# The first block's values taken from X before the norm, the normalised operand made beside them from the turned X

## The chip, the core and the metric

The kernel runs on one core of one Trainium2 chip. The metric is the device time of one execution, in microseconds (us). The kernel before took 1599.45 us, the median of three runs (1598.53 to 1599.94).

## The reference, cut to what matters

The network is a first block (mixer of mLSTM heads and a gated MLP, cross attention, a mixture of experts, final norm) followed by two layers of a second block, on 256 rows of 1024 numbers. All of the change lies in the first microseconds of the first block. There the reference computes

```
h    = x * rsqrt(mean(x*x, axis=-1) + eps) * g_mix      # 256 x 1024
proj = h @ w_in                                         # 1024 x PROJ_COLS
v    = proj[:, 1024:1536]                               # values, 4 heads of 128
gates = proj[:, 2048:2064]                              # and q, k, o, u, v of the gated MLP
```

The factor rsqrt(...) is one number for each row of x, so it can be taken out of the product: v = rsqrt(...) * ((x * g_mix) @ w_in).

## The kernel before, in words

Every engine has a program written out by hand; Python functions named after the engine emit it (tensor_mixer, scalar_mixer, vector_mixer, gpsimd_start, sync_start), and the order of the calls is the order of the work on that engine. Nothing reorders it. Engines wait on each other by counting semaphores (`e.wait_ge(*s.name[event])`). All instructions pass through a small class Port, so the profile shows its lines: L172 matmul, L175 transpose, L178 activation on ScalarE, L184 tensor_tensor, L187 tensor_scalar, L190 scalar_tensor_tensor, L217 a DMA issue. Groups are told apart by the names of tiles.

The weights come as a stream of chunks of 128 x 1024 numbers, two to a unit of 1 MB, from `in_ws_dram` into a ring of seven units (RING). A product in 32 bits is made of three reduced-precision ones. For this ScalarE copies each chunk, rounded, to WH ("hi", hi_half), and VectorE subtracts it from the chunk to give the rest in RINGL ("lo", lo_half); chunks 1 and 3 have their rest made on GpSimd (LOW_ON_POOL). The activations are split in the same way: HA (hi, from ScalarE) and LA (lo, from VectorE). TensorE then does hi*hi, hi*lo and lo*hi.

The first norm: the sum of squares of a tile of 128 rows is taken half on ScalarE (mean_square), half on VectorE (vector_square). VectorE adds them (rstd_mean), ScalarE takes log and exponential (rstd_root), VectorE does one Newton step in two instructions (rstd_step, rstd_last: the two `SM<-SM` of L190, together rstd_end) and puts the root on a diagonal matrix DIAG (rstd_diagonal). TensorE multiplies X by DIAG (norm_turn), which turns and normalises it at once, eight products for each tile t of 128 rows, four to a PSUM bank. norm_hi and norm_lo take HA and LA from these banks, with the gain g_mix as a scale by partition, from the parameters PARS.

The values (chunks 0 to 3) are computed in tiles: stream_tile(c0, j, t) is chunk j for rows t, six products of 512 columns. After the eight such groups come chunk 4 (the gates, stream_t: eight steps of three products of 256 columns), and chunk 5, before which TensorE also waits for the constants. From there on the stream of chunks goes on without a pause for a long time. SyncE issues the DMAs in one order (sync_start): X tile 0, the identity, PARS, unit 0, X tile 1, unit 1, unit 2, the memory, unit 3, the other constants, units 4 to 6; unit 7 and later wait for a chunk of the ring to be used up.

Chunks 0 and 1 are unit 0, chunks 2 and 3 unit 1, chunks 4 and 5 unit 2.

Of the kernel before, what the change touches and what calls it, by code (L numbers as in the profile page):

```python
# [38 lines left out]
_n = 0  # L39
for _name, _w in [("g_mix", 8), ("g_mem", 8), ("g_xattn", 8), ("g_moe", 8), ("conv_w", 40),  # L40
                  ("conv_b", 8), ("g_head", 4), ("gate_b", 1), ("br", 1),
# [598 lines left out]
def fetch(e, m, s, A, u):  # L640

    if u == U_B2:
        w = m.slot[m.home[u]]
        e.dma_start(w[:, 0:1024], A["ws"][u][:, 0:1024]).then_inc(*s.first_in.up(0))
# [284 lines left out]
def sync_start(e, m, s, A):  # L929
    e.dma_start(m.X[:, 0, :], A["x"][0]).then_inc(*s.x_in.up(0))  # L930
    e.dma_start(m.CONS[:, 0:128], A["con"][:, 0:128]).then_inc(*s.ident_in.up(0))
    e.dma_start(m.PARS[:, :], A["par"]).then_inc(*s.par_in.up(0))
# [42 lines left out]

def tensor_mixer(e, m, s):
    a = normed(s, "mix", m.HA, m.LA)
    norm_turn(e, m, s, "mix", m.X, 0)
    for j in range(3):
        stream_tile(e, m, s, 0, j, 0, a, None)  # L980
    norm_turn(e, m, s, "mix", m.X, 1)
    stream_tile(e, m, s, 0, 3, 0, a, (s.evac, ("v", 0)))
    for j in range(4):
        stream_tile(e, m, s, 0, j, 1, a, (s.evac, ("v", 1)))
# [421 lines left out]
def vector_mixer(e, m, s):  # L1406
# [12 lines left out]
    norm_lo(e, m, s, "mix", m.HA, m.LA, "g_mix", 0, 0)
    e.wait_ge(*s.x1_in[0])  # L1420
    vector_square(e, m, s, 1)
    norm_lo(e, m, s, "mix", m.HA, m.LA, "g_mix", 0, 1)
    lo_half(e, m, s, 2)
    e.wait_ge(*s.square["mix", 1, 0])
    e.wait_ge(*s.square_v[1])
    rstd_mean(e, m, s, "mix", 1)
    rstd_end(e, m, s, "mix", 1)
    rstd_diagonal(e, m, s, "mix", 1)
    lo_halves(e, m, s, 4, 6)
    norm_lo(e, m, s, "mix", m.HA, m.LA, "g_mix", 1, 0)  # L1430
    norm_lo(e, m, s, "mix", m.HA, m.LA, "g_mix", 1, 1)
# [3006 lines left out]
```

## Time and profile before

| what | value |
|---|---|
| median of three runs | 1599.45 us |
| time of the profiled execution | 1598.25 us |
| its span in the profile | 1596.4 us |
| TensorE busy with products | 1558.0 us (98%) |
| VectorE, ScalarE, GpSimd busy | 952.6, 692.8, 63.8 us |
| the chain that ended last | TensorE 84%, DMA 10%, VectorE 4%, ScalarE 2% |

The span is what the profile covers; the time of the same execution is 1.85 us longer. Busy time counts the time in which an engine works on an instruction. The chain is followed back from the last instruction to whatever released each step.

### The profile page before, as it was taken

The numbers are of one execution on the slowest core, as the hardware profiler recorded it, in microseconds if no ns is written. First come the engines' busy times: TensorE is split into PE (matmuls) and PEld (weight loads), VectorE is DVE, ScalarE is ACT, GpSimd is POOL, SyncE is SP. The second block draws the span as 40 slices with busy tenths as digits, with TensorE's granted clock in tenths as the row PEclk, the third lists the DMA queues.
The fourth block names the chain that finished last, engine by engine and source line by source line (L and its number), as shares of the span: only waits on it lengthen the run. The fifth ranks groups of instructions, "written<-read, shape, count | busy, mean of one in ns | idle before, by whom it ended". The sixth has DMA issues, their size and how long they took to land.

```text
span 1596.4 us, 22640 instructions
## 1 busy us (share of the span) xinstructions
PE 1558.0 (98%) x9209; PEld 1178.2 (74%) x9209; DVE 952.6 (60%) x1636; ACT 692.8 (43%) x1229; POOL 63.8 (4%) x68
## 2 busy tenths in 40 slices
PE   7999999999999999999999999999999999999998
PEld 6997885443433433448997889999899978899997
DVE  5967655222333233237788667766767885677666
ACT  6765542111010110136664446554655644465544
POOL 1010000000000000003001000000030010000000
PEclk9999999999999999999999999999999999999999
DMA  9443477999999999996345545555453445455550
GB/s 367 170 148 132 177 324 297 410 423 424 423 424 423 422 424 424 424 420 214 133 146 179 179 160 214 186 186 187 169 185 133 172 158 184 173 198 185 185 185 27
DMA packets 57246, 398.87 MB, mean 250 GB/s; under 512 B 6352, under 2 KB 6736, under 8 KB 10036
## 3 DMA queue, kind: packets, MB, share of 16 engines
q1 hardware_dynamic: 56706, 395.63, 64.2%
q8 instruction: 73, 1.20, 0.3%
q10 hardware_dynamic: 434, 1.77, 0.3%
q14 instruction: 33, 0.27, 0.1%
HBM read 396.33 MB, written 1.05 MB: 249 GB/s over the span
## 4 chain that ended last, share of the span: by engine, by line
PE 84%; DMA 10%; DVE 4%; ACT 2%; issue 1%; SPq 0%; DVEq 0%; ACTq 0%
PE P L172 82%; DMA ew<-in_ws_dram 8%; PE P L175 2%; DMA ez<-in_ws_dram 1%; DVE RINGL L184 1%; ACT WH L178 0%; DMA RING<-in_ws_dram 0%; DVE LA L190 0%; SPq L217 0%; ACT HA L178 0%; DVE SM L190 0%; DVE YB L184 0%; DVE PXP L190 0%; ACT JNK L178 0%; ACT L181 0%
## 5 line engine op out<-in xcount | busy, mean ns | idle before, releaser
L184 DVE TENSOR_TENSOR RINGL<-RING,WH 128x1024 fp32r<-128x1024 f32 x347 | 421.9, 1240 | 104.7 <-ACT WH L178 103.4
L178 ACT ACTIVATE WH<-RING 128x1024 fp32r<-128x1024 f32 x351 | 356.5, 1053 | 49.9 <-PE P L172 47.5
L172 PE MATMUL P<-HA,WH 128*128 128x256 f32 x1208 | 345.4, 286 | 0.0
L172 PE MATMUL P<-LA,WH 128*128 128x256 f32 x1208 | 340.3, 282 | 0.0
L172 PE MATMUL P<-HA,RINGL 128*128 128x256 f32 x1208 | 340.3, 282 | 0.0
L172 PEld LDWEIGHTS P<-HA,WH 128*128 128x128 f32 x1208 | 227.7, 189 | 5.6 <-issue 3.0
L172 PEld LDWEIGHTS P<-HA,RINGL 128*128 128x128 f32 x1208 | 228.4, 189 | 1.9
L172 PEld LDWEIGHTS P<-LA,WH 128*128 128x128 f32 x1208 | 228.6, 189 | 0.0
L172 PE MATMUL P<-WH,HA 128*128 128x512 f32 x368 | 148.1, 402 | 1.8 <-ACT VN L178 1.3
L172 PE MATMUL P<-RINGL,HA 128*128 128x512 f32 x368 | 145.7, 396 | 1.8 <-POOL RINGL L184 1.4
L172 PE MATMUL P<-WH,LA 128*128 128x512 f32 x368 | 144.9, 394 | 0.5 <-DVE LA L190 0.4
L172 PE MATMUL P<-RING,XT 128*64 128x512 f32 x536 | 122.3, 594 | 4.0 <-DMA RING<-in_ws_dram 4.0
L184 DVE TENSOR_TENSOR GS<-P,GS 128x512 f32<-128x512 f32 x16 | 11.1, 692 | 175.3 <-PE P L172 175.3
L172 PEld LDWEIGHTS P<-RING,XT 128*64 128x64 f32 x536 | 37.6, 137 | 82.5 <-issue 67.4
L190 DVE SCALAR_TENSOR_TENSOR YSL<-P,SM,YSH 128x512 fp32r<-128x512 f32 x32 | 22.6, 747 | 121.9 <-ACT YSH L178 121.9
L172 PEld LDWEIGHTS P<-WH,HA 128*128 128x128 f32 x368 | 69.4, 188 | 18.4 <-ACT WH L178 1.7
L172 PEld LDWEIGHTS P<-RINGL,HA 128*128 128x128 f32 x368 | 69.5, 189 | 18.0 <-POOL RINGL L184 1.8
L172 PEld LDWEIGHTS P<-WH,LA 128*128 128x128 f32 x368 | 69.3, 188 | 17.4 <-DVE LA L190 1.5
L172 PE MATMUL P<-ew,XT 128*64 128x512 f32 x304 | 71.4, 596 | 6.8 <-DMA ew<-in_ws_dram 6.8
L178 ACT ACTIVATE HT<-P 128x512 f32<-128x512 f32 x16 | 9.6, 598 | 155.9 <-PE P L175 155.9
L178 ACT ACTIVATE YSH<-P,SM 128x512 fp32r<-128x512 f32 x32 | 20.4, 684 | 130.7 <-PE P L172 130.7
L172 PE MATMUL P<-WH,FL 128*128 128x512 f32 x176 | 69.8, 396 | 0.0
(411 smaller groups left out, 2431.6 us busy)
## 6 DMA issues: line engine op xcount, KB each, us to landing
RING<-in_ws_dram SPq DMA_DIRECT2D x279, 1024.0 KB, 4.9
ew<-in_ws_dram SPq DMA_DIRECT2D x42, 1024.0 KB, 23.6
ez<-in_ws_dram SPq DMA_DIRECT2D x15, 1024.0 KB, 20.5
ek<-in_ws_dram SPq DMA_DIRECT2D x11, 1024.0 KB, 18.2
ef<-in_ws_dram SPq DMA_DIRECT2D x8, 1024.0 KB, 12.8
eha<-in_ws_dram SPq DMA_DIRECT2D x4, 1024.0 KB, 9.3
ela<-in_ws_dram SPq DMA_DIRECT2D x3, 1024.0 KB, 6.9
ewr<-in_ws_dram SPq DMA_DIRECT2D x3, 1024.0 KB, 13.8
```

The source lines that it names most:

```text
L172: return self.engine.matmul(*a, **k) if self.engine else self
L175: return self.engine.transpose(*a) if self.engine else self
L178: return self.engine.activation(*a, **k) if self.engine else self
L184: return self.engine.tensor_tensor(*a) if self.engine else self
L190: return self.engine.scalar_tensor_tensor(*a) if self.engine else self
```

## The change

The values are computed from X itself, turned with the identity (raw_turn, transposes instead of products with DIAG) and multiplied by the gain, split into HB and LB (first_hi, first_lo). The root is applied when the values leave PSUM, as a scale by partition (scalar_values). Both tiles are turned before chunk 1, and the groups of the values alternate between the tiles: v(0,0), turn of tile 1, v(1,0), v(0,1), v(1,1), v(2,0), spread, v(2,1), v(3,0), v(3,1).

All that follows (chunk 4 on) still reads the normalised HA and LA. They are now made from the same PSUM banks: two small products (spread_root) of a matrix of ones with DIAG put the roots of all 256 rows on every partition, ScalarE copies them to RB0, VectorE multiplies the turned X by gain and RB0 into QK (first_normal, 16 instructions in 4 groups), ScalarE rounds QK to HA (first_normal_hi, 4 instructions of 128 x 512), and GpSimd subtracts to give LA (first_normal_lo, 4 instructions of 128 x 512). Chunk 1's rest moves from GpSimd to VectorE; chunk 3's stays on GpSimd.

The gain moves from PARS to a place beside the identity, so both come in one DMA. Units 0 and 1 are fetched in halves, each chunk with a semaphore of its own; the ones (64 KB) and PARS come behind unit 1.

```diff
@@ sync_start @@
-    e.dma_start(m.CONS[:, 0:128], A["con"][:, 0:128]).then_inc(*s.ident_in.up(0))
-    e.dma_start(m.PARS[:, :], A["par"]).then_inc(*s.par_in.up(0))
+    e.dma_start(m.CONS[:, 0:136], A["con"][:, 0:136]).then_inc(*s.ident_in.up(0))
     fetch(e, m, s, A, 0)
     e.dma_start(m.X[:, 1, :], A["x"][1]).then_inc(*s.x1_in.up(0))
     fetch(e, m, s, A, 1)
+    e.dma_start(m.CONS[:, 136:264], A["con"][:, 136:264]).then_inc(*s.ones_in.up(0))
+    e.dma_start(m.PARS[:, :], A["par"]).then_inc(*s.par_in.up(0))
     fetch(e, m, s, A, 2)
...
@@ gpsimd_start @@
-    lo_half(e, m, s, 1)
     lo_half(e, m, s, 3)
+    first_normal_lo(e, m, s, 0, 0)
+    first_normal_lo(e, m, s, 1, 0)
+    first_normal_lo(e, m, s, 0, 1)
+    first_normal_lo(e, m, s, 1, 1)
@@ new functions @@
+def first_normal(e, m, s, t, i):
+    ta = slice(t * 128, (t + 1) * 128)
+    e.wait_ge(*s.evac["spread", "mix"])
+    for q in range(4):
+        k = 4 * i + q
+        p = e.scalar_tensor_tensor(m.QK[:, k, ta], m.P[4 + 2 * t + i][:, q * 128:(q + 1) * 128],
+                                   m.con("gain", k, k + 1), m.RB0[:, ta], ALU.mult, ALU.mult)
+    p.then_inc(*s.normal.up(t, i))
+def first_normal_hi(e, m, s, t, i):
+    ta = slice(t * 128, (t + 1) * 128)
+    e.wait_ge(*s.normal[t, i])
+    e.activation(m.HA[:, 4 * i:4 * i + 4, ta], m.QK[:, 4 * i:4 * i + 4, ta],
+                 ACT.Copy).then_inc(*s.norm_hi.up("mix", t, i))
+def first_normal_lo(e, m, s, t, i):
+    ta = slice(t * 128, (t + 1) * 128)
+    e.wait_ge(*s.norm_hi["mix", t, i])
+    e.tensor_tensor(m.LA[:, 4 * i:4 * i + 4, ta], m.QK[:, 4 * i:4 * i + 4, ta],
+                    plain(m.HA[:, 4 * i:4 * i + 4, ta]), ALU.subtract).then_inc(*s.normal_lo.up(t, i))
...
@@ tensor_mixer @@
+    raw_turn(e, m, s, "mix", 0, [(s.x_in, (0,))] * 2)
+    v(0, 0)
+    raw_turn(e, m, s, "mix", 1, [(s.x1_in, (0,))] * 2)
...
+    v(2, 0)
+    e.wait_ge(*s.ones_in[0])
+    spread_root(e, m, s, "mix", 3)
+    v(2, 1)
+    v(3, 0)
+    v(3, 1)
+    a = Operand(m.HA, m.LA, lambda k, t: (s.norm_hi, ("mix", t, k // 4)), lambda k, t: (s.normal_lo, (t, k // 4)))
     stream_t(e, m, s, 4, a, (s.evac, ("gate", 3)))
@@ scalar_mixer @@
+    first_hi(e, m, s, 0, 0)
+    hi_halves(e, m, s, 0, 2)
+    first_hi(e, m, s, 0, 1)
     mean_square(e, m, s, "mix", 0, 0)
+    e.wait_ge(*s.x1_in[0])
+    e.wait_ge(*s.square["mix", 0, 0])
+    mean_square(e, m, s, "mix", 1, 0)
+    first_hi(e, m, s, 1, 0)
+    rstd_root(e, m, s, "mix", 0)
+    rstd_root(e, m, s, "mix", 1)
+    hi_half(e, m, s, 2)
+    first_hi(e, m, s, 1, 1)
+    hi_halves(e, m, s, 3, 5)
+    e.wait_ge(*s.product["spread", "mix", 1])
+    e.activation(m.RB0[:, :], m.P[m.bank["spread", "mix"]][:, 0:256], ACT.Copy).then_inc(*s.evac.up("spread", "mix"))
+    hi_half(e, m, s, 5)
+    first_normal_hi(e, m, s, 0, 0)
+    first_normal_hi(e, m, s, 1, 0)
+    scalar_values(e, m, s, 0)
+    first_normal_hi(e, m, s, 0, 1)
+    first_normal_hi(e, m, s, 1, 1)
+    hi_half(e, m, s, 6)
+    scalar_values(e, m, s, 1)
+    hi_halves(e, m, s, 7, 9)
@@ scalar_values @@
+    e.wait_ge(*s.scale["mix", t])
     e.activation(m.V1[:, t, :, 0:128], m.P[m.bank[0, t]][:, :].rearrange("p (h d) -> p h d", h=4),
-                 ACT.Copy).then_inc(*s.evac.up("v", t))
+                 ACT.Copy, scale=m.SM[:, 12 + t:13 + t]).then_inc(*s.evac.up("v", t))
@@ vector_mixer @@
     vector_square(e, m, s, 0)
+    first_lo(e, m, s, 0, 0)
+    lo_halves(e, m, s, 0, 2)
+    first_lo(e, m, s, 0, 1)
...
+    vector_square(e, m, s, 1)
...
+    first_lo(e, m, s, 1, 0)
+    lo_half(e, m, s, 2)
+    for t in range(2):
+        rstd_end(e, m, s, "mix", t)
+        vector_scale(e, m, s, "mix", t)
+        rstd_diagonal(e, m, s, "mix", t)
+    first_lo(e, m, s, 1, 1)
+    lo_half(e, m, s, 4)
+    first_normal(e, m, s, 0, 0)
+    first_normal(e, m, s, 1, 0)
+    first_normal(e, m, s, 0, 1)
+    first_normal(e, m, s, 1, 1)
     e.wait_ge(*s.par_in[0])
-    lo_half(e, m, s, 0)
...
+    lo_half(e, m, s, 5)
     lo_halves(e, m, s, 6, 10)
```

What GpSimd has at the start of its program before, behind five memsets (RINGL is a chunk's rest, GV belongs to a much later part):

```order
L214 MEMSET NC 128x512
L184 ISA
L184 TENSOR_TENSOR RINGL<-RING,WH 128x1024 [waits hi] x2
L184 TENSOR_TENSOR GV<-GV,LNG 128x512 [waits ln_g_in,vec]
L184 TENSOR_TENSOR GV<-GV,LNB 128x512 [waits gained,ln_b_in]
```

And now:

```order
L214 MEMSET NC 128x512
L184 ISA
L184 TENSOR_TENSOR RINGL<-RING,WH 128x1024 [waits hi]
L184 TENSOR_TENSOR LA<-QK,HA 128x4x128 [waits norm_hi] x4
L184 TENSOR_TENSOR GV<-GV,LNG 128x512 [waits ln_g_in,vec]
L184 TENSOR_TENSOR GV<-GV,LNB 128x512 [waits gained,ln_b_in]
```

One of the two subtractions of a chunk has left, and four of half the size, on the operand of chunk 4, stand behind the other.

VectorE from the rest of chunk 2 to the rest of chunk 5 in the changed kernel (SM<-SM are the steps of the root, tile 0 and then tile 1):

```order
L184 TENSOR_TENSOR RINGL<-RING,WH 128x1024 [waits hi]
L190 SCALAR_TENSOR_TENSOR SM<-SM 128x1 [waits root]
L190 SCALAR_TENSOR_TENSOR SM<-SM 128x1 [waits rstd]
L187 TENSOR_SCALAR SM<-SM 128x1 [waits rstd]
L187 TENSOR_SCALAR DIAG<-CONS,SM 128x128
L190 SCALAR_TENSOR_TENSOR SM<-SM 128x1 [waits root]
L190 SCALAR_TENSOR_TENSOR SM<-SM 128x1 [waits rstd]
L187 TENSOR_SCALAR SM<-SM 128x1 [waits rstd]
L187 TENSOR_SCALAR DIAG<-CONS,SM 128x128
L190 SCALAR_TENSOR_TENSOR LB<-P,CONS,HB 128x128 [waits norm_hi]
L190 SCALAR_TENSOR_TENSOR LB<-P,CONS,HB 128x128 x3
L184 TENSOR_TENSOR RINGL<-RING,WH 128x1024 [waits hi]
L190 SCALAR_TENSOR_TENSOR QK<-P,CONS,RB_90 128x128 [waits evac]
L190 SCALAR_TENSOR_TENSOR QK<-P,CONS,RB_90 128x128 x15
L184 TENSOR_TENSOR RINGL<-RING,WH 128x1024 [waits hi,par_in]
```

Both roots now stand together, and behind them wait the rest of tile 1's second half, the rest of chunk 4 and the sixteen products that make the normalised operand; before, the second root stood behind the rest of chunk 2, and two subtractions of chunks and eight instructions of LA followed it.

## Rows read from the trace of the kernel before

**Rows 1.** The page: busy time, share of the span, instructions.
```profile
PE 1558.0 (98%) x9209; PEld 1178.2 (74%) x9209; DVE 952.6 (60%) x1636; ACT 692.8 (43%) x1229; POOL 63.8 (4%) x68
```
**Rows 2.** Chain of waits, in order: start us, us, what.
```profile
19.12 60.86 PE P L172 x438
...
428.28 26.48 DMA ew<-in_ws_dram
```
**Rows 3.** Who waited for whom on SyncE's DMA queue, whole span: total, times, longest.
```profile
SPq L217 <- PE P L172: 1344.5, 348, 15.0
```
**Rows 4.** Timeline of TensorE, first 29 us: start, length, instruction, [idle before <-releaser].
```profile
7.42 3.79 PE L172 MATMUL P<-DIAG,X 128*128 128x128 f32 x16 [7.42 <-DVE DIAG L187]
...
12.39 0.63 PE L172 MATMUL P<-WH,HA 128*128 128x512 f32 x1
...
12.82 0.59 PE L172 MATMUL P<-RINGL,HA 128*128 128x512 f32 x1
...
15.24 0.50 PE L172 MATMUL P<-RINGL,HA 128*128 128x512 f32 x1 [1.38 <-POOL RINGL L184]
...
19.12 2.05 PE L172 MATMUL P<-DIAG,X 128*128 128x128 f32 x16 [1.04 <-DVE DIAG L187]
```
**Rows 5.** Stretches: us, TensorE's busy time (instructions), clock, DMA share, GB/s.
```profile
28.01:30.87 2.86, 2.86 (x25) 1.00 0.99 370
```
**Rows 6.** SyncE's timeline at 1.2 us; DMA issues from 1.1 to 1.6: KB, us to landing.
```profile
1.18 0.42 SPq L217 DMA_DIRECT2D CONS<-in_con_dram  x1
...
CONS<-in_con_dram SPq DMA_DIRECT2D x1, 64.0 KB, 3.1
```
**Rows 7.** Timeline, transposes with the identity at 174 us.
```profile
173.93 1.47 PE L175 MATMUL P<-CONS,X 128*128 128x128 f32 x12
```
**Rows 8.** Timeline of ScalarE, VectorE and GpSimd, 6 to 23 us.
```profile
6.16 0.44 ACT L178 ACTIVATE SM<-SM 128x1 f32<-128x1 f32 x2 [1.21 <-DMA PARS<-in_par_dram]
...
6.63 0.41 DVE L190 SCALAR_TENSOR_TENSOR SM<-SM 128x1 f32<-128x1 f32 x2 [1.29 <-ACT SM L178]
...
8.94 1.06 ACT L178 ACTIVATE WH<-RING 128x1024 fp32r<-128x1024 f32 x1 [2.34 <-DMA RING<-in_ws_dram]
...
9.90 1.13 ACT L178 ACTIVATE HA<-P,PARS 128x128 fp32r<-128x128 f32 x4
10.10 1.22 DVE L184 TENSOR_TENSOR RINGL<-RING,WH 128x1024 fp32r<-128x1024 f32 x1 [2.73 <-ACT WH L178]
...
11.24 1.12 DVE L190 SCALAR_TENSOR_TENSOR LA<-P,PARS,HA 128x128 fp32r<-128x128 f32 x4
...
11.51 1.07 ACT L178 ACTIVATE WH<-RING 128x1024 fp32r<-128x1024 f32 x1
...
12.66 2.53 POOL L184 TENSOR_TENSOR RINGL<-RING,WH 128x1024 fp32r<-128x1024 f32 x1 [10.29 <-ACT WH L178]
...
22.61 0.60 ACT L178 ACTIVATE V<-P 128x512 f32<-128x512 f32 x1
```
**Rows 9.** Timeline of GpSimd and VectorE side by side, at 15 and 109 us.
```profile
15.58 2.94 POOL L184 TENSOR_TENSOR RINGL<-RING,WH 128x1024 fp32r<-128x1024 f32 x1 [0.39 <-ACT WH L178]
...
16.90 1.84 DVE L190 SCALAR_TENSOR_TENSOR SM<-SM 128x1 f32<-128x1 f32 x2 [0.50 <-ACT SM L178]
...
109.33 1.50 POOL L184 TENSOR_TENSOR GV<-GV,LNG 128x512 f32<-128x512 f32 x1 [90.80 <-DVE GV L187]
...
109.62 2.29 DVE L184 TENSOR_TENSOR RINGL<-RING,WH 128x1024 fp32r<-128x1024 f32 x1
...
110.97 2.08 POOL L184 TENSOR_TENSOR GV<-GV,LNB 128x512 f32<-128x512 f32 x1
...
111.83 1.11 DVE L190 SCALAR_TENSOR_TENSOR MN<-P,COLS,CONS 128x128 f32<-128x128 f32 x4
...
113.02 1.29 POOL L184 TENSOR_TENSOR GV<-GV,LNG 128x512 f32<-128x512 f32 x1
```
**Rows 10.** All copies of a row of roots from PSUM (tile RB): ns min/median/max.
```profile
L178 ACT ACTIVATE RB<-P x4: 377/378/378, 736.6 to 1414.4; 128x256 f32<-128x256 f32 x4
```

More of the change, by code:

```diff
@@ L39 @@
 _n = 0
-for _name, _w in [("g_mix", 8), ("g_mem", 8), ("g_xattn", 8), ("g_moe", 8), ("conv_w", 40),
+for _name, _w in [("g_mem", 8), ("g_xattn", 8), ("g_moe", 8), ("conv_w", 40),
                   ("conv_b", 8), ("g_head", 4), ("gate_b", 1), ("br", 1),
@@ L53 @@
 _n = 0
-for _name, _w in [("ident", 128), ("ones", 128), ("le", 128), ("ge", 128), ("lt", 128),
+for _name, _w in [("ident", 128), ("gain", 8), ("ones", 128), ("le", 128), ("ge", 128), ("lt", 128),
                   ("mf", 128), ("mb", 128), ("onehot", 512), ("iota", 64), ("cf", 130), ("cb", 130),
@@ L253 @@
 XS = 256 ** -0.5
-CON_WIDTH = {"iota": 64, "onehot": 512, "cf": 130, "cb": 130, "m2": 64, "edge": 64, "lrone": 1}
-LOW_ON_POOL = {1, 3} | {B2 + l * L_CHUNKS + L_AT["ffn"] + 12 for l in range(2)}
+CON_WIDTH = {"iota": 64, "onehot": 512, "cf": 130, "cb": 130, "m2": 64, "edge": 64, "gain": 8, "lrone": 1}
+LOW_ON_POOL = {3} | {B2 + l * L_CHUNKS + L_AT["ffn"] + 12 for l in range(2)}
 EXTRA = ("ek1", "egs", "ez", "ef2", "ef1", "ext", "eha", "ela", "ew0", "ew1", "ew2", "ewr")
@@ L363, in __init__ @@
         self.DN = z("DN", [128, 4])
+        self.RB0 = z("RB0", [128, 128 * 2])
         self.QX = at("QX", [128, 4, 256], Z + 16384)
@@ L602, in __init__ @@
         self.scaled = signal("scaled")
+        self.normal = signal("normal")
+        self.normal_lo = signal("normal_lo")
+        self.ones_in = signal("ones_in", 16)
+        self.second_in = signal("second_in", 16)
         self.norm_lo = signal("norm_lo")
@@ L640, in fetch @@
 def fetch(e, m, s, A, u):
[L642 removed]
+    if u in (0, 1, U_B2):
         w = m.slot[m.home[u]]
[L644 removed]
+        e.dma_start(w[:, 0:1024], A["ws"][u][:, 0:1024]).then_inc(*(s.second_in if u == 1 else s.first_in).up(u))
         e.dma_start(w[:, 1024:2048], A["ws"][u][:, 1024:2048]).then_inc(*s.landed[m.home[u]].up(u))
@@ L805, in norm_lo, with first_hi, first_lo @@
                                plain(hi[:, k, ta]), ALU.mult, ALU.subtract).then_inc(*s.norm_lo.up(tag, t, k))
+def first_hi(e, m, s, t, i):
+    e.wait_ge(*s.turned["raw mix", t, i])
+    for q in range(4):
+        k = 4 * i + q
+        e.activation(m.HB[:, k, t * 128:(t + 1) * 128], m.P[4 + 2 * t + i][:, q * 128:(q + 1) * 128], ACT.Copy,
+                     scale=m.con("gain", k, k + 1)).then_inc(*s.norm_hi.up("raw mix", t, k))
+def first_lo(e, m, s, t, i):
+    ta = slice(t * 128, (t + 1) * 128)
+    e.wait_ge(*s.norm_hi["raw mix", t, 4 * i + 3])
+    for q in range(4):
+        k = 4 * i + q
+        e.scalar_tensor_tensor(m.LB[:, k, ta], m.P[4 + 2 * t + i][:, q * 128:(q + 1) * 128], m.con("gain", k, k + 1),
+                               plain(m.HB[:, k, ta]), ALU.mult, ALU.subtract).then_inc(*s.norm_lo.up("raw mix", t, k))
+def first_normal(e, m, s, t, i):
+    ta = slice(t * 128, (t + 1) * 128)
+    e.wait_ge(*s.evac["spread", "mix"])
+    for q in range(4):
+        k = 4 * i + q
+        p = e.scalar_tensor_tensor(m.QK[:, k, ta], m.P[4 + 2 * t + i][:, q * 128:(q + 1) * 128],
[7 more added lines that the diff above has]
+def first_normal_lo(e, m, s, t, i):
+    ta = slice(t * 128, (t + 1) * 128)
+    e.wait_ge(*s.norm_hi["mix", t, i])
+    e.tensor_tensor(m.LA[:, 4 * i:4 * i + 4, ta], m.QK[:, 4 * i:4 * i + 4, ta],
+                    plain(m.HA[:, 4 * i:4 * i + 4, ta]), ALU.subtract).then_inc(*s.normal_lo.up(t, i))
 def normed(s, tag, hi, lo):
@@ L976, in tensor_mixer @@
 def tensor_mixer(e, m, s):
[L977 to L984, printed above, removed]
+    raw = normed(s, "raw mix", m.HB, m.LB)
+    v = lambda j, t: stream_tile(e, m, s, 0, j, t, raw, (s.evac, ("v", t)))
+    e.wait_ge(*s.ident_in[0])
+    raw_turn(e, m, s, "mix", 0, [(s.x_in, (0,))] * 2)
+    v(0, 0)
+    raw_turn(e, m, s, "mix", 1, [(s.x1_in, (0,))] * 2)
+    for t in range(2):
+        for i in range(2):
+            m.free[4 + 2 * t + i] = [(s.normal, (t, i))]
+    v(1, 0)
+    v(0, 1)
+    v(1, 1)
+    v(2, 0)
[5 more added lines that the diff above has]
+    a = Operand(m.HA, m.LA, lambda k, t: (s.norm_hi, ("mix", t, k // 4)), lambda k, t: (s.normal_lo, (t, k // 4)))
     stream_t(e, m, s, 4, a, (s.evac, ("gate", 3)))
@@ L1410, in vector_mixer @@
     vector_square(e, m, s, 0)
-    e.wait_ge(*s.ident_in[0])
-    e.wait_ge(*s.square["mix", 0, 0])
+    first_lo(e, m, s, 0, 0)
+    lo_halves(e, m, s, 0, 2)
+    first_lo(e, m, s, 0, 1)
+    e.wait_ge(*s.x1_in[0])
     e.wait_ge(*s.square_v[0])
-    rstd_mean(e, m, s, "mix", 0)
-    rstd_end(e, m, s, "mix", 0)
-    rstd_diagonal(e, m, s, "mix", 0)
-    e.wait_ge(*s.par_in[0])
-    lo_half(e, m, s, 0)
[L1419 to L1431, printed above, removed]
+    vector_square(e, m, s, 1)
+    for t in range(2):
+        e.wait_ge(*s.square["mix", t, 0])
+        e.wait_ge(*s.square_v[t])
+        rstd_mean(e, m, s, "mix", t)
+    first_lo(e, m, s, 1, 0)
+    lo_half(e, m, s, 2)
+    for t in range(2):
+        rstd_end(e, m, s, "mix", t)
[7 more added lines that the diff above has]
+    first_normal(e, m, s, 1, 1)
+    e.wait_ge(*s.par_in[0])
+    lo_half(e, m, s, 5)
     lo_halves(e, m, s, 6, 10)
@@ L1439, in vector_mixer @@
         rstd_end(e, m, s, "mem", t)
-        rstd_diagonal(e, m, s, "mem", t, (s.turned, ("mix", t, 1)))
+        rstd_diagonal(e, m, s, "mem", t, (s.product, ("spread", "mix", t)))
     lo_half(e, m, s, 11)
@@ L4383, in vec @@
         par[:v.shape[0], PAR[name]:PAR[name] + v.shape[1]] = v
-    for n in ("g_mix", "g_mem", "g_xattn", "g_moe", "g_head", "conv_w", "conv_b"):
+    con = constants()
+    con[:, CON["gain"]:CON["gain"] + 8] = I["g_mix"][0].reshape(8, 128).T
+    for n in ("g_mem", "g_xattn", "g_moe", "g_head", "conv_w", "conv_b"):
         vec(n, I[n][0])
```

21 lines of the change are left out of this document (3 added, 18 removed).

## The prediction

> **What bounds the kernel now.** First the page: TensorE works 98% of the span, VectorE 60%, GpSimd 4% [rows 1]. An average hides where the change lies, so next the chain of waits. From 19.12 us one piece of 60.86 us hangs on TensorE alone, 438 products without a wait [rows 2]. Whatever makes TensorE enter that piece earlier or later moves all behind it. Further on the chain holds pieces of DMA, such as the 26.48 us at 428 us [rows 2]; but the queue that issues these transfers waits, over the span, 348 times and 1344.5 us for TensorE [rows 3], so a shift at the start moves the transfers too and is neither absorbed nor enlarged there. So the question is one number: when does chunk 5 begin. Chunk 4 takes from 28.01 to 30.87 us, 24 products, 0.119 us each [rows 5]. Chunk 5 now begins at 30.87.
>
> Before that the timeline of TensorE shows the waste that could be won [rows 4]: nothing until 7.42; then products at the low clock, 0.43 us apart for 512 columns (12.39 to 12.82), which is 1.2 GHz, though the clock column of the profile reads 1.00; waits of 1.38 us for GpSimd's rest of chunk 1 and 1.04 us for the second DIAG. At the high level the two turns and 48 products (0.234 us each) need about 15 us of the 20.6 from 7.42 to 28.01.
>
> **The change, step by step.** I follow the new order with durations of the old rows.
>
> *TensorE's start.* The identity is issued at 1.18 and lands 3.1 us later [rows 6]: transposes from 4.3 instead of 7.42. Twelve transposes take 1.47 us, of which the last one's own length is pipelined, so some 0.11 each [rows 7]; at the low level 1.85 times as much, as the two turns of [rows 4] stand to each other (3.79 against 2.05 us): 0.21. The first four are done at 5.15, and another engine sees them some 0.25 later: 5.4. Units in halves and PARS moved behind cost nothing: the first half of unit 0 is needed at 6.4, and lies 1.1 MB behind the queue's start where before the whole unit with PARS lay 1.8 MB behind it and was used at 8.94 [rows 8]; if it came as late as that, the next steps would be 2.5 us later, which I keep as an outer bound. X tile 1, issued right behind, has until 11.0.
>
> *To the second turn.* ScalarE takes four copies of a quarter in 1.0 (9.90 to 10.90; HB like HA): 6.4. It starts chunk 0's rounding, VectorE starts the rest 1.16 after that (8.94 to 10.10 [rows 8]), 7.6, and TensorE can use it 1.3 later: 8.9. Five products at 0.43: 11.05. The second turn's first half and the handover, 0.84 + 0.25: 12.15.
>
> *To the roots.* ScalarE: four copies, 13.2; two roots at 0.46 (row at 6.16 [rows 8]), 14.1; rounding of chunk 2 from 14.1; four copies; rounding of chunk 3 from 16.15. VectorE: rest of chunk 2 from 14.1 + 1.16 = 15.25, for 1.14 (10.10 to 11.24), to 16.4. Then both roots, each two small steps (0.41 [rows 8]) and the scale and diagonal (0.45, from the stretch between the steps and 7.42 plus 0.2 for one more small instruction). The last step of the second root is due at 17.5.
>
> *Where it collides.* GpSimd starts chunk 3's rest 1.15 after ScalarE starts its rounding (11.51 to 12.66 [rows 8]): 17.3, for 2.53. In [rows 9] a small step SM<-SM that came at 16.90 in the middle of such a subtraction (15.58 to 18.52) ran until both were over: 1.84 us for what takes 0.41. So the second root's last step waits until 19.85, and TensorE gets its DIAG at 20.6, having finished v(2,0) before 19. The two products of the spread are four passes of 0.11; with handover and the copy to RB0 (0.38 [rows 10]) the row of roots is there at 21.7. That is hidden: VectorE, from 20.5, has four instructions of LB (1.04: 11.24 to 12.28) and the rest of chunk 4 (1.14) first. The sixteen products of the normalised operand start at 22.7.
>
> *Two engines for one operand.* Each group of four takes 1.04: ends at 23.75, 24.8, 25.8, 26.85. They read PSUM and one tile of SBUF and run beside GpSimd unharmed (MN at 111.83 [rows 9]: 1.11 for four). ScalarE needs 0.6 for 512 columns (V [rows 8]), so GpSimd starts at 24.55. Its piece of 512 takes 1.29 (113.02 [rows 9]); two end at 27.2. VectorE comes with chunk 5's rest at 26.85. In [rows 9] VectorE's rest at 109.62 waited for GpSimd's end at 110.83 and took 2.29 instead of 1.22, then GpSimd's next waited for VectorE and took 2.08 instead of 1.29: they take turns. Hence: VectorE 27.2 to 28.3; GpSimd's third, 29.5; chunk 6's rest, whose rounding ended at 28.6, 30.6; GpSimd's fourth, 31.8. Step 5 of chunk 4 needs it: 10 of the 24 products are left from 31.9, 1.2 us, and **chunk 5 begins at 33.1 instead of 30.87: 2.2 us later**.
>
> *The rest.* The scale on the copy of the values changes no shape: nothing, hidden anyway, since the bank is needed much later. The spread's products and RB0 are counted. Chunk 1's rest on VectorE (1.14) is in the stretch to 11.05, hidden behind TensorE's turn. Behind chunk 5 ScalarE and VectorE have slack as before.
>
> **Sum.** The profiled execution took 1598.25, 1596.4 of it span; with 2.2 more it would be 1600.5. It lies 1.2 below the median of the three runs, so I add to the median: 1599.45 + 2.2 = **1601.7**. Unknown prices at both ends: a piece of LA on GpSimd, which no row shows, lies between 1.15 (the 2.08 row less its wait until 111.9) and 1.5 (the 109.33 row), taken 1.2 to 1.3 from the nearest; at 1.5 all four come 1.0 later, 1602.7, and half a us more if VectorE wins another turn; the order at 17.3 against 17.5 is close: if the small step comes first, DIAG is there at 18.1, but chunk 4's rest, with both inputs in SBUF, waits for GpSimd until 20.2, and all comes only 1.3 earlier: +0.9. The forecast's own range is thus 1600.3 to 1603.2.
>
> **Rivals.**
> *A, slower: the clock falls back.* In the forecast TensorE waits 1.5 us at chunk 4's first step (25.7 to 27.2), then from 28.9 to 31.9. In [rows 4] waits of 1.38 and 1.04 left it at the high level (the second turn took 2.05). It decides whether the wait at step 5 grows to about 3 us. At the start the low level lasted from 7.42 to a little after 12.82, which cost half of that, 2.9; so a fall costs 1.2 (the rest of chunk 4 alone) to 2.9. With 2.3 in between: 1604.0. For it: the longest wait, three in a row (one before the spread too). Against it: no row shows a fall. The Trainium skill's page "TensorE: Matmul & The Clock Gate", section on HAM oscillation, says that waits between bursts of products throw the clock back to half; its Part 4 adds that transposes do not count as work in the same way, which speaks against this change. By that rule the time would be that of this case; no row here shows either.
> *B, about 2 faster: the two engines do not hold each other up.* Then the second DIAG is there at 18.1, the sixteen products start at 20.3 behind chunk 4's rest, GpSimd's four pieces run from 22.15, 1.37 apart, to 27.6, and chunk 5 begins at 28.9: 2.0 earlier, 1597.5. For it: the change gives GpSimd only pieces of half the size. Against it: all three meetings in [rows 9]. The Trainium skill's page "SBUF — State Buffer", section on the two separate sides, has the pair of ports as an exclusive lock taken by whichever starts first; by it this case is out, and the rows agree.
> *C, faster: the operand is ready when TensorE comes.* TensorE alone: from 12.7, 42 products and the spread, 10.3 us, chunk 4 at 23.0, chunk 5 at 25.9: 5 less, 1594.5. For it: it is what is left if TensorE sets the pace, as it does in 98% of the span. Against it: VectorE's and ScalarE's queues add up to 24.5 for the first HA alone.
>
> **Chances.** What a measurement can tell from no change is 0.2%, 3.2 us. Forecast 0.58, of which 0.11 beyond +3.2 (pieces on GpSimd dearer, one more turn of the two engines); A 0.17; B 0.15, of which 0.02 beyond -3.2; C 0.10. So faster 0.12, same 0.60, slower 0.28. The range 1597.4 to 1604.4 takes in B and the middle of A and leaves out C and A's upper half, some 0.18.
>
> **What the profile after would show.** Right: first product at 4.3; GpSimd's chunk 3 at about 17.3 and, inside it, a pair SM<-SM of over 2 us; TensorE idle before the spread; four LA on GpSimd with subtractions RINGL on VectorE in between, each longer than 1.3; TensorE waiting for LA at chunk 4; chunk 5 at about 33. A is seen as products of 256 columns more than 0.2 apart behind such a wait. B is seen as LA pieces of 1.3 in a row beside RINGL of 1.2. The forecast is wrong if chunk 5 begins before 31, or if it begins at 33 and the end does not move with it.

## The result

The changed kernel takes 1603.05 us (median of 13 runs, 1601.5 to 1605.33), the kernel before 1599.45 (13 runs, 1597.96 to 1600.35): ratio 1.0025, 95% interval 1.0018 to 1.0032. That is 3.6 us slower, where 2.2 had been forecast, and a little past the 0.2% (3.2 us) that the prediction took as the least that can be told from no change. The profiled execution took 1603.05 us, 1601.2 of it span. That is 4.8 more than the span before, whose execution lay 1.2 below its median.

The chain of waits of the changed kernel shows where it went (start us, us, what):

```profile
1.66 6.66 DMA RING<-in_ws_dram
...
8.34 1.06 ACT WH L178
...
9.42 1.24 DVE RINGL L184
...
18.97 2.35 DVE SM L190
...
22.72 1.13 DVE RINGL L184
23.85 1.05 DVE QK L190 x4
...
24.92 0.64 ACT HA L178
25.56 0.07 issue
25.63 6.95 POOL LA L184 x4
32.58 0.14 issue
32.72 51.74 PE P L172 x378
```

The long piece on TensorE alone, which began at 19.12 before [rows 2], now begins at 32.72, with 10 products of chunk 4 left. GpSimd, which did not appear on the chain before, holds 6.95 us of it. Chunk 5 starts at 34.99 instead of 30.87 [rows 5].

VectorE, the same timeline as in [rows 8, 9]:

```profile
18.01 0.41 DVE L190 SCALAR_TENSOR_TENSOR SM<-SM 128x1 f32<-128x1 f32 x2
...
18.72 2.58 DVE L190 SCALAR_TENSOR_TENSOR SM<-SM 128x1 f32<-128x1 f32 x2
...
23.77 4.22 DVE L190 SCALAR_TENSOR_TENSOR QK<-P,CONS,RB 128x128 f32<-128x128 f32 x16
27.91 1.31 DVE L184 TENSOR_TENSOR RINGL<-RING,WH 128x1024 fp32r<-128x1024 f32 x1
29.64 5.15 DVE L184 TENSOR_TENSOR RINGL<-RING,WH 128x1024 fp32r<-128x1024 f32 x3 [0.41 <-ACT WH L178]
```

And GpSimd:

```profile
18.89 2.40 POOL L184 TENSOR_TENSOR RINGL<-RING,WH 128x1024 fp32r<-128x1024 f32 x1 [16.53 <-ACT WH L178]
25.63 6.94 POOL L184 TENSOR_TENSOR LA<-QK,HA 128x512 fp32r<-128x512 f32 x4 [4.34 <-ACT HA L178]
```

The first root's pair of small steps takes 0.41, the second's 2.58, and ends when GpSimd's piece ends (21.29). The 2.35 us of the line DVE SM in the chain are thus mostly a wait for GpSimd. It was close: GpSimd's piece began at 18.89, the step that it held up at 18.97. The four pieces of LA take 6.94, and VectorE's three rests beside them 5.15 instead of 3.5 (an estimate from e6, where four take 4.63).

TensorE, the same timeline as in [rows 4]:

```profile
4.40 1.97 PE L175 MATMUL P<-CONS,X 128*128 128x128 f32 x8 [4.40 <-DMA CONS<-in_con_dram]
9.44 0.79 PE L172 MATMUL P<-WH,HB 128*128 128x512 f32 x1 [3.07 <-ACT WH L178]
...
21.74 0.49 PE L172 MATMUL P<-DIAG,CONS 128*128 128x128 f32 x2 [0.78 <-DVE DIAG L187]
...
28.29 0.36 PE L172 MATMUL P<-LA,WH 128*128 128x256 f32 x1 [1.09 <-POOL LA L184]
...
32.72 0.55 PE L172 MATMUL P<-LA,WH 128*128 128x256 f32 x1 [2.76 <-POOL LA L184]
33.07 0.41 PE L172 MATMUL P<-HA,WH 128*128 128x256 f32 x1
33.28 0.41 PE L172 MATMUL P<-HA,RINGL 128*128 128x256 f32 x1
```

TensorE starts 3.0 us earlier, and then waits 3.07 us, until 9.44, for chunk 0's rounding. After the wait of 2.76 the products are 0.21 apart instead of 0.12. The clock column of the stretch 32.72 to 35.42 says the same (columns: TensorE busy (instructions), clock, DMA share, GB/s):

```profile
32.72:35.42 2.70, 2.70 (x13) 0.50 1.01 420
```

The granted clock was 0.50, the level of 1.2 GHz: rival A's mechanism, on top of the forecast's.

### The profile page after: what moved, and what is told of

It is laid out like the page before. It is cut to its first block, busy times and chain, and to the rows that moved or that the text cites. A ratio compares the mean times of both kernels' runs of the same rounds, so it can differ in the third digit from the quotient of the medians.

```text
span 1601.2 us, 22652 instructions
## 1 busy us (share of the span) xinstructions
PE 1559.7 (97%) x9197; PEld 1178.2 (74%) x9197; DVE 959.8 (60%) x1655; ACT 695.1 (43%) x1234; POOL 67.6 (4%) x71
## 4 chain that ended last, share of the span: by engine, by line
PE 83%; DMA 10%; DVE 4%; ACT 2%; issue 1%; POOL 0%; SPq 0%; DVEq 0%; ACTq 0%
PE P L172 81%; DMA ew<-in_ws_dram 8%; PE P L175 2%; DVE RINGL L184 1%; DMA ez<-in_ws_dram 1%; ACT WH L178 0%; POOL LA L184 0%; DMA RING<-in_ws_dram 0%; SPq L217 0%; DVE SM L190 0%; DVE LA L190 0%; DVE YB L184 0%; DVE PXP L190 0%; ACT L181 0%; ACT HA L178 0%
## 5 line engine op out<-in xcount | busy, mean ns | idle before, releaser
L172 PE MATMUL P<-WH,HA 128*128 128x512 f32 x352 | 141.1, 401 | 1.7 <-ACT VN L178 1.3
L172 PE MATMUL P<-RINGL,HA 128*128 128x512 f32 x352 | 138.8, 394 | 0.5 <-DVE RINGL L184 0.5
L172 PE MATMUL P<-WH,LA 128*128 128x512 f32 x352 | 138.3, 393 | 0.5 <-DVE LA L190 0.4
L172 PEld LDWEIGHTS P<-WH,HA 128*128 128x128 f32 x352 | 66.1, 188 | 17.7 <-ACT WH L178 1.7
L172 PEld LDWEIGHTS P<-RINGL,HA 128*128 128x128 f32 x352 | 66.2, 188 | 15.2 <-DVE RINGL L184 0.9
## 6 DMA issues: line engine op xcount, KB each, us to landing
ew<-in_ws_dram SPq DMA_DIRECT2D x42, 1024.0 KB, 23.7
```

The lines of the kernel that those rows point to most:

```text
L172: return self.engine.matmul(*a, **k) if self.engine else self
```

## The experiments

The landing of unit 0's first half differs from execution to execution, though the DMA issues are the same, and moves all that follows. So in this table the end of LA is counted from the start of chunk 0's rounding on ScalarE, which is given as a time of the profile, like the start of chunk 5. Times in us; "LA" is the end of the last piece of the operand; each ratio is against runs of the kernel before on the same chip.

The three columns of times come from one profiled execution for each kernel, the median from 5 to 13 runs. The profiled one was not always typical: of its 11 runs it was the fastest for e1 (1598.98), and the slowest for e2 (1602.76), e6 (1600.34) and e10 (1600.38).

| kernel | rounding starts | LA ends, from there | chunk 5 starts | median | ratio (95%) |
|---|---|---|---|---|---|
| before | 8.94 | | 30.88 | 1599.45 | |
| changed | 8.34 | 24.2 | 34.99 | 1603.05 | 1.0025 (1.0018 to 1.0032) |
| e1 | 6.93 | 23.2 | 31.55 | 1602.7 | 1.0016 (1.0007 to 1.0025) |
| e2 | 9.32 | 22.1 | 34.53 | 1601.05 | 1.0010 (1.0001 to 1.0019) |
| e3 | 8.69 | 21.0 | 33.42 | 1600.4 | 1.0003 (0.9994 to 1.0012) |
| e4 | 7.76 | 22.3 | 31.44 | 1600.12 | 1.0004 (0.9995 to 1.0013) |
| e5 | 9.50 | 24.3 | 36.16 | 1604.76 | 1.0037 (1.0024 to 1.0051) |
| e6 | 8.52 | 19.4 | 29.59 | 1597.99 | 0.9992 (0.9983 to 1.0001) |
| e7 | 9.01 | | 31.28 | 1599.74 | 1.0005 (0.9996 to 1.0014) |
| e8 | 8.90 | 24.1 | 34.44 | 1602.04 | 1.0022 (1.0013 to 1.0031) |
| e9 | 9.28 | 24.0 | 34.70 | 1604.91 | 1.0038 (1.0024 to 1.0051) |
| e10 | 8.94 | | 31.04 | 1599.03 | 0.9996 (0.9987 to 1.0005) |
| e11 | 9.04 | 18.2 | 28.93 | 1596.08 | 0.9982 (0.9973 to 0.9991) |

**e1, chunk 3's rest on VectorE**

```diff
-LOW_ON_POOL = {3} | ...
+LOW_ON_POOL = set() | ...
... gpsimd_start
-    lo_half(e, m, s, 3)
... vector_mixer
     first_lo(e, m, s, 1, 1)
+    lo_half(e, m, s, 3)
     lo_half(e, m, s, 4)
```

> The changed kernel with the rest of chunk 3 made on VectorE (before that of chunk 4), so that GpSimd is idle while the second root is finished. Theory (GpSimd's subtraction holds up VectorE's small step SM<-SM): the pair at 18.7 us takes 0.41 instead of 2.58, VectorE has 1.14 more to do, so the sixteen products of the normalised operand start near 22.7 instead of 23.77, chunk 5 starts about 1.1 us earlier, time 1602.0. Rival (the 2.58 us have another cause, such as the wait for ScalarE's root): they stay, the products start at 24.9, 1604.2.

VectorE of this kernel:

```profile
17.32 0.41 DVE L190 SCALAR_TENSOR_TENSOR SM<-SM 128x1 f32<-128x1 f32 x2
...
21.32 4.22 DVE L190 SCALAR_TENSOR_TENSOR QK<-P,CONS,RB 128x128 f32<-128x128 f32 x16
```

The second pair takes 0.41. Counted from chunk 0's rounding the sixteen products start 14.4 us later here and 15.4 in the changed kernel: the 1.1 that was expected. The theory held in the trace. The median (1602.7, expected 1602.0) shows it only weakly: set against the kernel before on its own chip it is 2.8 slower instead of 3.6.

TensorE of this execution, behind its longest wait:

```profile
30.29 0.36 PE L172 MATMUL P<-LA,WH 128*128 128x256 f32 x1 [2.77 <-POOL LA L184]
30.48 0.28 PE L172 MATMUL P<-HA,WH 128*128 128x256 f32 x1
```

The wait is as long as in the changed kernel, and the clock held (products 0.12 apart). The other ten runs of e1 had a lower granted clock over the whole execution (0.995 to 0.998; the profiled one 0.999), so a part of the 1.1 may have been lost to it in them; no trace of those runs shows where.

**e2, LA on VectorE**

```diff
-    first_normal_lo(e, m, s, 0, 0)      # GpSimd; and the other three
...
     first_normal(e, m, s, 1, 1)
+    first_normal_lo(e, m, s, 0, 0)      # VectorE; and the other three
```

> The changed kernel with all four subtractions that make LA on VectorE, behind its sixteen products and before the rest of chunk 5. Theory (the four pieces on GpSimd, in turns with VectorE's rests, set the end of chunk 4): products end at 27.9, four pieces of some 0.62 us each (half of a rest of 1.22) end at 30.4, TensorE's longest wait shrinks to about 2.3 us and the clock stays up, chunk 5 starts near 31.9 instead of 35.6: time 1599.4. Rival (what counts is the late start of the products, on whatever engine LA is made): no more than 1 us earlier, 1602.

```profile
28.90 2.48 DVE L184 TENSOR_TENSOR LA<-QK,HA 128x512 fp32r<-128x512 f32 x4
```

Four pieces in 2.48, 0.62 each as estimated, and behind all sixteen products they are still complete 2.2 us earlier than GpSimd's, which had started while VectorE was still at its products. The median is 1.65 above the expected 1599.4. The expectation had the clock stay up; in the profiled execution (1602.76) 17 products at 0.21 spacing follow the wait of 2.13 at chunk 4, and chunk 0 came 1.0 later than in the changed kernel's profile. How much of the median is due to either is not shown.

**e3, both of them**

The edits of e1 and e2 together.

> Both of the edits together: nothing of the first stage on GpSimd. Theory of the shared port: the two gains add, products from 22.7, LA complete near 29.3, chunk 5 from 30.8 as in the kernel before, time 1598.3 to 1599. Rival (VectorE is the bound and every move onto it costs what it weighs, 1.14 plus 2.5): chunk 5 at 34 or later, 1602 or more.

Counted from the rounding, LA is complete 3.3 us earlier than in the changed kernel, and e1 and e2 give 1.0 and 2.2 alone: they add, so the rival falls. Chunk 5 starts at 33.42, not 30.8: TensorE's wait of 2.13 was followed by products at 0.21 (27 of them). The median of 1600.4 lies above the expected 1598.3 to 1599 and below the rival's 1602.

```profile
28.59 0.55 PE L172 MATMUL P<-LA,WH 128*128 128x256 f32 x1 [2.13 <-DVE LA L184]
28.94 0.41 PE L172 MATMUL P<-HA,WH 128*128 128x256 f32 x1
29.16 0.41 PE L172 MATMUL P<-HA,RINGL 128*128 128x256 f32 x1
```

**e4, the same work, VectorE waiting for LA before chunk 5's rest**

```diff
     e.wait_ge(*s.par_in[0])
+    e.wait_ge(*s.normal_lo[1, 1])
     lo_half(e, m, s, 5)
```

> The changed kernel in which VectorE waits for the last LA before it makes the rest of chunk 5. It does the same work on the same engines. Theory (the two engines take turns on one port, and TensorE's 2.8 us wait lets the clock fall): GpSimd's four pieces take 5.5 instead of 6.94 us, end at 31.1, TensorE waits 1.4 instead of 2.8 us and stays at the high level, chunk 5 starts near 32.4 when its rest is ready, 3.2 earlier: time about 1600. If the clock falls all the same: 1601. Rival (GpSimd's pieces are slow by themselves, 1.7 us each): they end at 32.6 as before and chunk 5 waits for its rest until 33.8 or more: 1603 to 1604.

```profile
25.04 4.99 POOL L184 TENSOR_TENSOR LA<-QK,HA 128x512 fp32r<-128x512 f32 x4 [4.34 <-ACT HA L178]
```

One more wait makes the kernel faster: the four pieces take 4.99 instead of 6.94, 1.25 each, so GpSimd is not slow by itself. TensorE's last wait is 0.81, no product behind it is at 0.21, and the median is 1600.12, a ratio (1.0004) whose interval lies below the changed kernel's. Counted from the rounding, chunk 5 starts 23.7 later instead of 26.65: 1.95 of that is the pieces, the rest that the clock held. This is the cleanest evidence for the turns, since nothing but the order of two engines differs.

**e5, units 0 and 1 whole again**

```diff
-    if u in (0, 1, U_B2):
+    if u == U_B2:
```

> The changed kernel with units 0 and 1 fetched whole again; PARS and the ones stay behind unit 1. In the five profiles of the changed start the first half of unit 0 arrives between 6.9 and 9.3 us. Theory (arrival of chunk 0 leads all that follows, and halving brings it only some 0.8 us earlier than the whole unit, since the second half landed 0.8 behind the first): the rounding of chunk 0 starts 0.8 to 1.3 us later, time 1603.9 to 1604.4. Rival (halving costs more in the queue than it brings): chunk 0 arrives at the same time or earlier, 1603 or less.

Chunk 0's rounding starts at 9.50, 1.2 later than in the changed kernel's profile and later than in any profile with halves. The median of five runs, 1604.76, is a little above the expected range; the lowest of them, 1603.49, is above the changed kernel's median. Against the kernel before on the same chip it is 5.6 slower instead of 3.6. So the halves are worth some 2 us to this kernel.

**e6, fewer meetings of VectorE and GpSimd**

```diff
... tensor_mixer
-    v(2, 0)
     spread_root(e, m, s, "mix", 3)
+    v(2, 0)
... gpsimd_start
-    lo_half(e, m, s, 3)
-    first_normal_lo(e, m, s, 0, 1)
-    first_normal_lo(e, m, s, 1, 1)
... vector_mixer (the loop shortened)
     first_lo(e, m, s, 1, 0)
+    for t in range(2): rstd_end, vector_scale, rstd_diagonal
     lo_half(e, m, s, 2)
-    for t in range(2): rstd_end, vector_scale, rstd_diagonal
     first_lo(e, m, s, 1, 1)
+    lo_half(e, m, s, 3)
     lo_half(e, m, s, 4)
...
     first_normal(e, m, s, 1, 1)
+    first_normal_lo_v(e, m, s, 0, 1)    # the same on VectorE, with its own semaphore
+    first_normal_lo_v(e, m, s, 1, 1)
```

> An attempt at a better one: the changed kernel with the rest of chunk 3 on VectorE, both roots finished before the rest of chunk 2, the spread before v(2,0), the first two LA pieces on GpSimd (beside VectorE's products, which read PSUM) and the last two on VectorE. Theory of the port: LA is complete some 19.6 us after the rounding of chunk 0 starts (24.2 in the changed kernel, 21.0 with nothing on GpSimd), chunk 5 starts 21.2 after it (21.9 in the kernel before), time 1598 to 1599, at or below the kernel before. Rival (VectorE's own work, or the arrival of chunk 0, sets the end): no better than with nothing on GpSimd, 1600.4.

LA after 19.4, chunk 5 21.07 after the rounding: as expected. The median is the expected one and 5 us below the changed kernel; against the kernel before the interval just touches 1.

**e7, the kernel before with units 0 and 1 in halves**

```diff
-    if u == U_B2:
+    if u in (0, 1, U_B2):
```

> The kernel before with one part of the change alone: units 0 and 1 in halves with a semaphore for each chunk. Theory: chunk 0 is there 0.8 us sooner (about 8.1 instead of 8.9), but the rests of chunk 1 on GpSimd and of the second root are what TensorE waits for, so 0.3 to 0.8 earlier: 1599.0 to 1599.5. Rival (more transfers in the queue delay each other): the same or up to 1 us later, 1599.9 to 1600.9.

The rounding starts at 9.01, no earlier than before: here PARS (208 KB) still lies ahead of it. No gain is seen: the median is 0.6 above that of the kernel before on the same chip, and the interval takes in no change. That fits the rival, not the theory. The DIAG of tile 0 comes 0.7 later in this profile (first product at 8.16 instead of 7.42), since the root waits for PARS, which was seen 0.7 later.

**e8, twenty filler products in TensorE's longest wait**

```diff
             e.matmul(out, lo[:, w], a.hi[:, k, :], start=False, stop=False)
+            if c == 4 and k == 4:
+                e.wait_ge(*s.evac["spread", "mix"])
+                for f in range(20):
+                    e.matmul(m.P[m.bank["spread", "mix"]][:, 0:256], hi[:, w], a.hi[:, 0, :], start=f == 0, stop=f == 19)
```

> The changed kernel with 20 products of 256 columns (2.4 us) into an unused bank placed in TensorE's wait of 2.8 us for the third and fourth pieces of LA; their result is thrown away. Theory (this wait lets the clock fall in some executions, as in the profile of the changed kernel, where 14 products after it were 0.21 us apart): the clock never falls after it, the profile shows 0.12 us between the products of the rest of chunk 4, median 0.3 to 1.2 lower than the changed kernel's 1603.05: 1602.3. Rival (the fall has nothing to do with the wait): products at 0.21 appear all the same, 1603 or more.

```profile
30.21 2.54 PE L172 MATMUL P<-HA,WH 128*128 128x256 f32 x20
33.18 0.35 PE L172 MATMUL P<-LA,WH 128*128 128x256 f32 x1 [0.42 <-POOL LA L184]
33.37 0.28 PE L172 MATMUL P<-HA,WH 128*128 128x256 f32 x1
33.49 0.28 PE L172 MATMUL P<-HA,RINGL 128*128 128x256 f32 x1
```

LA is as late as in the changed kernel (24.1), yet chunk 5 starts 25.5 after the rounding instead of 26.65, and the products are 0.12 apart. That is what the theory expected, but it does not show that the fillers did it: e1 and e9 have no fillers, waited 2.77 at the same place, and their chunk 4 also ran on at 0.12. In e9 the fall came later, 1.4 us behind the end of the wait, while TensorE was working, and cost about 1.5 us behind the start of chunk 5 that the table does not show (columns as in the stretch of the changed kernel):

```profile
33.43:34.82 1.39, 1.39 (x12) 1.00 0.99 413
34.82:38.15 3.33, 3.33 (x18) 0.51 0.58 236
```

The median is 1.0 lower, 0.7 when each is set against the kernel before on its own chip, and the two intervals overlap. What speaks for the theory is the granted clock over whole executions: 0.999 in 7 of 11 runs and never 0.997, against 2 of 13 and 3 of 13 in the changed kernel. That the fillers keep the clock up is likely, not shown.

**e9, PARS ahead of unit 0 again**

```diff
+    e.dma_start(m.PARS[:, :], A["par"]).then_inc(*s.par_in.up(0))
     fetch(e, m, s, A, 0)
...
-    e.dma_start(m.PARS[:, :], A["par"]).then_inc(*s.par_in.up(0))
     fetch(e, m, s, A, 2)
```

> The changed kernel with PARS (204 KB) fetched at its old place, ahead of unit 0. Theory (moving it behind bought next to nothing: between 4 and 6 us the transfers run at 160 to 240 GB/s with PARS there or not): chunk 0's rounding starts within the spread of the other profiles (6.9 to 9.3, 8.3 in the changed kernel), at most 0.5 later on average, 1603.0 to 1603.6. Rival (the 1.9 us between the landings of the identity and of PARS in the kernel before are PARS's own): 1.5 to 1.9 later, 1604.5 to 1605.

By the time my theory falls: all five runs (1604.28 to 1606.32) are above the changed kernel's median, and the median, 1604.91, is the rival's (5.5 above the kernel before on the same chip, instead of 3.6). The rounding alone, at 9.28, would not decide it, since it lies within the spread that the theory allowed. So moving PARS behind does help, by some 2 us.

**e10, the lesson of e1 on the kernel before**

```diff
-LOW_ON_POOL = {1, 3} | ...
+LOW_ON_POOL = {1} | ...
... gpsimd_start
-    lo_half(e, m, s, 3)
... vector_mixer
     rstd_diagonal(e, m, s, "mix", 1)
-    lo_halves(e, m, s, 4, 6)
+    lo_halves(e, m, s, 3, 5)
...
-    lo_halves(e, m, s, 6, 10)
+    lo_halves(e, m, s, 5, 10)
```

> The kernel before with the rest of chunk 3 on VectorE behind the second DIAG (and that of chunk 5 behind the last LA), so that GpSimd no longer works when the second root is finished. Theory of the port: the pair SM<-SM at 16.9 takes 0.41 instead of 1.84, DIAG comes 1.4 earlier, TensorE's wait of 1.04 goes; VectorE has 1.14 more to do behind it, and LA of tile 1 may take back half: chunk 5 starts 0.5 to 1.3 earlier, 1598.1 to 1598.9. Rival (no lock, or VectorE is the bound): 1599.4 or up to 1 us more.

```profile
16.89 0.41 DVE L190 SCALAR_TENSOR_TENSOR SM<-SM 128x1 f32<-128x1 f32 x2 [0.51 <-ACT SM L178]
17.34 0.29 DVE L187 TENSOR_SCALAR DIAG<-CONS,SM 128x128 f32<-128x128 f32 x1
```

The pair that took 1.84 in [rows 9] takes 0.41 and DIAG is there 1.4 earlier, but TensorE turns tile 1 at 19.46, not at 18. The reason is the clock:

```profile
15.24 0.76 PE L172 MATMUL P<-RINGL,HA 128*128 128x512 f32 x1 [1.98 <-POOL RINGL L184]
15.79 0.63 PE L172 MATMUL P<-WH,LA 128*128 128x512 f32 x1
```

```profile
15.24:17.20 1.96, 1.96 (x5) 0.52 1.04 431
```

The wait for GpSimd's rest of chunk 1 ended at 15.24, as before, but the products behind it ran 0.43 apart until 18.35, at a granted clock of 0.52, where they had been 0.23 apart. At 0.23 the eleven products before the turn would have been done at about 17.9 (an estimate), just behind DIAG. Chunk 5 starts at 31.04 in this, the slowest of the 11 runs, and the median is within the uncertainty of the kernel before. So the hold-up of the small steps by GpSimd is shown once more; what its removal is worth here is open.

**e11, chunk 3's rest on GpSimd beside products that read PSUM**

```diff
 # on e6
+    lo_half(e, m, s, 3)                 # GpSimd, ahead of first_normal_lo
...
-    lo_half(e, m, s, 3)                 # VectorE
-    lo_half(e, m, s, 4)
     first_normal(e, m, s, 0, 0)         # and the other three
+    lo_half(e, m, s, 4)
```

> The better one (both roots early, the last two LA pieces on VectorE) with the rest of chunk 3 back on GpSimd, now beside VectorE's products that read PSUM, and the rest of chunk 4 behind these. Theory (GpSimd may work freely while VectorE reads PSUM): VectorE has 1.14 less ahead of the products, they start at about 20.3 instead of 22.35, chunk 5 starts at 28.9 to 29.2 instead of 29.6: 1597.3 to 1597.7. Rival (GpSimd's piece collides with the rest of chunk 2 or 4 again): 1598 or more.

VectorE's sixteen products, and GpSimd:

```profile
20.52 4.23 DVE L190 SCALAR_TENSOR_TENSOR QK<-P,CONS,RB 128x128 f32<-128x128 f32 x16
```

```profile
19.35 2.42 POOL L184 TENSOR_TENSOR RINGL<-RING,WH 128x1024 fp32r<-128x1024 f32 x1 [16.98 <-ACT WH L178]
22.39 2.56 POOL L184 TENSOR_TENSOR LA<-QK,HA 128x512 fp32r<-128x512 f32 x2 [0.62 <-ACT HA L178]
```

GpSimd's two stretches (19.35 to 21.77 and 22.39 to 24.95) lie almost wholly beside VectorE's products (20.52 to 24.75) and, ahead of these, its four LB (19.32 to 20.44), which read PSUM too. All take what they take alone: 4.23 (4.22 in e1), 2.42 (2.40 in the changed kernel) and 2.56 (1.28 a piece; 1.25 in e4). The last 0.28 of GpSimd's second stretch meets VectorE's next rest, which takes 1.37 instead of 1.22. Chunk 5 starts 19.9 after the rounding, 2.1 sooner than before. 1596.08 us beats both kernels: 3.3 below the kernel before (0.9982, at most 0.9991), 7 below the changed one. The median came out better than the expected 1597.3 to 1597.7. Since two pieces moved at once (the rests of chunks 3 and 4 both left the place ahead of the products), the gain over e6 is that of the pair.

## Why the prediction held, and where it was off

The direction, the two places where VectorE and GpSimd hold each other up, and the range (1597.4 to 1604.4) were right. By its steps:

- *TensorE's start*: 4.3 forecast, 4.40 seen. Right, and worth nothing here, since chunk 0's arrival came later than ScalarE was ready for it (it waited 1.55).
- *Chunk 0's arrival*: wrong. It was taken to be there by 6.4; its rounding started at 8.34, with an issue at 1.66. The forecast had counted the 1.1 MB ahead and kept "2.5 us later" as an outer bound, of which 1.9 came true. Between 4 and 6 us the transfers ran at 164 and 197 GB/s. Nor was it this one execution: in the eight profiles with these DMA issues the rounding started between 6.93 and 9.32, 8.4 on average, and never by 6.4. e5 and e9 show that both DMA edits help; together they brought it only from 8.94 to 8.34 in the profile.
- *The second root behind GpSimd*: right. Forecast 2.3 us of delay, seen 2.17 (2.58 less 0.41); e1 removes it. The prediction had called the order close (17.3 against 17.5), and it was: 18.89 against 18.97. It came out the same way in every kernel that left chunk 3's rest on GpSimd in that place (e2, e4, e5, e8, e9: the pair takes 2.56 to 2.59).
- *The sixteen products* start at 23.77 instead of 22.7, only 1.1 late. The other 0.9 of chunk 0's delay was not slack, for the chain has no gap there; the steps between were forecast too long: 10.55 from the rounding to GpSimd's piece (10.9 forecast), 2.40 for that piece (2.53), and 0.31 from its end to the next LB (0.65).
- *The turns for LA*: right. From the start of the products to the end of LA 9.1 was forecast, 8.8 seen; e4 takes 1.95 of it away without moving work. TensorE's two waits at chunk 4 were forecast at 1.5 and 3.0 and were 1.09 and 2.76.
- *Chunk 5* starts at 34.99 instead of 33.1: 1.1 from the late start, -0.3 from LA, 1.1 from the clock (2.27 us from 32.72, where 1.2 was counted).
- *The clock*: given to rival A with 0.17, it happened in the profiled execution and cost 1.1 before chunk 5 and about 0.4 after it, below the 2.3 that A put on it. It does not happen in every run (e1), and it can come on top of all that the forecast has. So the forecast and A should not have been alternatives, but one sum with a chance of the fall in it. The Trainium skill ("TensorE: Matmul & The Clock Gate", HAM oscillation) has the rule that waits between bursts halve the clock; the trace agrees here (0.50 in the stretch), and e1, with a wait of 2.77 and the clock at 1.00 behind it, does not.
- *To the end*: the last GU of the first block moves from 103.6 to 108.1, 4.5, and the span by 4.8. In this pair of executions the shift is neither absorbed nor enlarged, as said.

That the time came within 1.4 us of the forecast owes something to luck: chunk 0's delay of 1.9 and the clock's 1.5 came on top, and steps forecast too long took back 0.9 and 0.3; and the profiled execution before lay 1.2 below its median.

Rival B is out (e1, e4). Rival C is out: the operand was complete 6.2 us after TensorE had finished the values' last product at 26.4.

## What to carry to other kernels

Before work is moved between VectorE and GpSimd, look at what each reads: operations of VectorE with both inputs in SBUF and GpSimd's subtractions ran only one after the other here, down to an instruction of one column (2.35 us in the changed kernel), while those that read PSUM ran beside it at no cost (4.23 against 4.22 us for sixteen products). Put GpSimd's pieces next to the latter (e11), and nothing small and urgent beside them. And an earlier start of the leading engine is worth only what the next arrival allows: here TensorE's first instruction came 3 us earlier, and it then waited 3 us for the first weights. Last, see where the profiled execution stands among the runs before its waits are taken for those of the kernel: those of e1 and e10 were the fastest and the slowest of 11, and in one the clock held where in the other it fell.

## What was not expected of the hardware

- The landing of the same transfer moves by more than 2 us between executions: with the same DMA issues (changed kernel, e1 to e4, e6, e8, e11) chunk 0's rounding started between 6.93 and 9.32. The kernel before and its two variants stand at 8.94, 9.01 and 8.94. Why is open.
- Whether the clock falls is not set by the length of the wait alone: after 2.77 us it held (e1, products 0.12 apart behind it), after 2.76 and 2.78 it fell (changed kernel, e5), after another 2.77 it fell only 1.4 us behind the end of the wait (e9), and after 2.13 and 1.98 it fell too (e2, e3, e10).
- Between 104 and 687 us the distance between two executions can change by 2 us and more: e6 had its last GU 1.3 us before that of the kernel before, and its GpSimd copy of the filter at 684.3 against 683.1. In that stretch the 16 DMA engines are busy throughout (share 1.01, 421 GB/s from 270 to 530 us before and 418 in e6); whether this is the cause was not tried.
